# A two-block transformer kernel in fp32: the second feed-forward stage's output products by token tile, and h kept by token from there on

## The reference

```python
# first block
h = h + 0.5 * rmsnorm(swiglu(rmsnorm(h, g0), W_in0, W_out0), g1)     # stage "f0", inner width 2816
u = rmsnorm(h, g2)
h = h + rmsnorm(mlstm_mixer(u), g3)                                  # mixer "a", 8 heads
h = h + 0.5 * rmsnorm(swiglu(rmsnorm(h, g4), W_in1, W_out1), g5)     # stage "f1"; the 16 tokens are dropped
# second block, twice (layers 0 and 1)
shift, scale, gate = split(silu(c) @ w_ada[l] + b_ada[l])            # the modulation
u = rmsnorm(h, pre[l]) * (1 + scale) + shift
q, k, v, gates and convolution inputs = u @ w_in[l]
mix = concat(attention(q, k, v) * silu(g), short_conv(...) * silu(g2))
h = h + gate * rmsnorm(mix @ w_out[l], post[l])
```

## Time and profile before

| | |
|---|---|
| median of 3 runs | 803.59 us (802.58 to 805.04) |
| the profiled execution | 803.42 us, of it the span 801.6 us |
| PE, DVE, ACT, POOL busy | 791.0, 589.6, 419.3, 141.9 us |
| f1's output products, in the span | 469.07 to 530.32 us |
| boundary to layer 0's first product | 530.32 to 536.00 us |
| layer 0's query and key blocks, then values | 536.00 to 559.64, to 570.86 us |
| layer 0's output products, with the first tile's return | 640.89 to 666.37 us |
| layer 1's values, then query and key blocks | 666.37 to 680.80, to 703.58 us |

### The profile page before, as it was taken

How to read it: one execution, slowest core, us unless ns; L and a number is a source line. 1 busy time by engine, 2 the same in 40 slices (tenths; PEclk the granted TensorE clock), 3 DMA queues, 4 the chain that set the end, 5 groups by cost and what they waited for, 6 DMA issues and landing times.

```text
span 801.6 us, 15412 instructions
## 1 busy us (share of the span) xinstructions
PE 791.0 (99%) x6215; PEld 761.6 (95%) x6215; DVE 589.6 (74%) x938; ACT 419.3 (52%) x724; POOL 141.9 (18%) x155
## 2 busy tenths in 40 slices
PE   9999999999999999999999999999999999999997
PEld 9999999999999999999999999999899987999985
DVE  6877777699687976778777779996576667566753
ACT  7544444444358575555444455446546447556541
POOL 3800000042320000020000003330154411034510
PEclk9999999999899999999999999999999999999999
DMA  9876667695426642648867769555453560754531
GB/s 323 311 257 240 217 245 247 209 328 176 140 85 220 200 145 80 184 158 294 304 218 247 252 232 341 174 174 185 154 169 125 183 237 25 239 158 126 157 113 53
DMA packets 45190, 158.83 MB, mean 198 GB/s; under 512 B 5040, under 2 KB 6576, under 8 KB 45120
## 3 DMA queue, kind: packets, MB, share of 16 engines
q1 hardware_dynamic: 45120, 157.85, 59.4%
HBM read 156.76 MB, written 1.06 MB: 197 GB/s over the span
## 4 chain that ended last, share of the span: by engine, by line
PE 87%; DVE 9%; issue 2%; ACT 1%; POOL 0%; DVEq 0%; POOLq 0%; ACTq 0%
PE ps L334 24%; PE ps L336 23%; PE ps L335 23%; DVE w L1157 3%; PE ps L708 2%; DVE acc L1175 1%; PE ps L350 1%; PE ps L771 1%; PE ps L769 1%; PE ps L770 1%; PE ps L608 1%; PE ps L387 1%; PE ps L679 1%; PE ps L698 1%; PE ps L688 1%
## 5 line engine op out<-in xcount | busy, mean ns | idle before, releaser
L1157 DVE TENSOR_TENSOR w<-raw,w 128x1024 fp32r<-128x1024 f32 x241 | 295.9, 1240 | 136.3 <-ACT w L814 136.0
L334 PE MATMUL ps<-u,w 128*128 128x256 f32 (+1 forms) x1259 | 361.2, 287 | 0.6 <-DVE w L1157 0.6
L336 PE MATMUL ps<-u,w 128*128 128x256 f32 (+1 forms) x1259 | 357.6, 284 | 0.0
L335 PE MATMUL ps<-u,w 128*128 128x256 f32 (+1 forms) x1259 | 357.1, 284 | 0.0
L814 ACT CAST w<-raw 128x1024 fp32r<-128x1024 f32 x241 | 250.0, 1050 | 117.6 <-PE ps L336 103.4
L334 PEld LDWEIGHTS ps<-u,w 128*128 128x128 f32 x1259 | 237.5, 189 | 6.9 <-issue 4.3
L336 PEld LDWEIGHTS ps<-u,w 128*128 128x128 f32 x1259 | 237.8, 189 | 0.0
L335 PEld LDWEIGHTS ps<-u,w 128*128 128x128 f32 x1259 | 237.1, 188 | 0.0
L334 PE MATMUL ps<-h,w 128*128 128x272 f32 (+1 forms) x352 | 99.8, 283 | 0.0
L335 PE MATMUL ps<-h,w 128*128 128x272 f32 (+1 forms) x352 | 99.4, 282 | 0.0
L336 PE MATMUL ps<-h,w 128*128 128x272 f32 (+1 forms) x352 | 99.2, 282 | 0.0
(11 more groups left out here) (257 smaller groups left out, 957.3 us busy)
## 6 DMA issues: line engine op xcount, KB each, us to landing
raw<-wst SPq DMA_DIRECT2D x245, 512.0 KB, 4.6
adr<-wada SPq DMA_DIRECT2D x48, 512.0 KB, 4.1
Bt<-bias_rows SPq DMA_DIRECT2D x8, 192.0 KB, 3.9
hT<-xT SPq DMA_DIRECT2D x4, 272.0 KB, 5.4
outT<-hT SPq DMA_DIRECT2D x4, 256.0 KB, 2.0
cs<-cst SPq DMA_DIRECT2D x1, 140.0 KB, 6.4
cs<-cst SPq DMA_DIRECT2D x1, 128.0 KB, 6.9
vc<-vec SPq DMA_DIRECT2D x1, 101.0 KB, 3.6
```

What stands on the lines that cost most here:

```text
L334: e.matmul(out, a, x1, start=first, stop=False)
L335: e.matmul(out, a, x2, start=False, stop=False)
L336: return e.matmul(out, b, x1, start=False, stop=last)
L1157: e.tensor_tensor(b, raw[:, k % NRAW, :], a.bitcast(F32), ALU.subtract).then_inc(*tick(s_split, k))
```

## The change

f1's outputs are made by `token_outputs`, as a layer's are: the 22 blocks of the inner width are the stationary operand, 128 tokens at a time, and the rows of the second weight move, 512 columns in each half. 17 chunks are used for both token tiles, the last five in two passes. `ada_sums(1)` stands behind chunk 13, h is turned behind chunks 16 and 19. DVE's part of it is `second_ffn_out`, with the ten modulation steps and three folds at fixed chunks. The column sums, spreads and POOL's squares of f1 go, and with them `both_scales` and `normalised` of f1. `next_input` serves both boundaries. h is by token from f1's end; at layer 0's end it is read from SBUF (`ygf`) and not turned again. `attention(0)` now begins with its values, as `attention(1)` does; their four chunks are loaded inside f1's last chunks and lie in a new place, `side[0]`, over buffers of f1's modulation. Gain rows are made elsewhere: layer 0's `G2` in the boundary behind f0, f1's gains behind the mixer, both in the place of fillers; layer 1's `G2` at layer 0's start.

```diff
-        C_QK, C_G, C_V = (165, 209), (177, 217), ((173, 174, 175, 176), (202, 204, 206, 208))
-        C_OUT = ((197, 198, 199, 200, 201, 203, 205, 207), tuple(range(237, 245)))
+        C_QK, C_G, C_V = (169, 209), (177, 217), ((162, 164, 166, 168), (202, 204, 206, 208))
+        C_OUT = {"f1": (*range(143, 162), 163, 165, 167), "l0": (*range(197, 202), 203, 205, 207), "l1": (*range(237, 245),)}
...
-            def both_scales(s, n, rows_of_gains=False):
+            def both_scales(s, n):
...
                 spread(("r1", s), 6, n, rst)
-                if rows_of_gains:
-                    gain_rows(0, 1)
-                    rows_of_g2(0)
-                else:
-                    dense(6)
+                rows_of_g2(0, 0, 7)
+                dense(2)
                 e.wait_ge(s_pow.handle, at(s_pow, ("r2", s)))
                 spread(("r2", s), 5, n, rst2)
-                if rows_of_gains:
-                    dense(2)
-                    rows_of_g2(1)
+                dense(2)
+                rows_of_g2(0, 1, 4)
...
                 keys = [("in", 1, i) for i in range(2 * NF)]
-                head(keys[:4], C_F[1], x1, x2, S, *u_of("f1"), hook=spread_scale)
+                gain_rows("f1", 0, 7)
+                dense(2)
+                gain_rows("f1", 1, 4)
+                head(keys[:4], C_F[1], x1, x2, S, *u_of("f1"), fill=0, hook=spread_scale)
...
-                if l == 0:
-                    head(keys[:4], C_QK[0], x1, x2, S, *u_of("l0"), fill=0)
...
+                s = ("f1", "l0")[l]
+                values_of(0)
+                for half in range(2):
+                    gain_rows(("l0", "l1")[l], half)
                 if l == 0:
+                    rows_of_g2(1, 0, 4)
+                rows_to_features(s, 1, 0)
+                rows_to_features(s, 1, 1)
+                if l == 0:
+                    rows_of_g2(1, 1, 7)
+                values_of(1, 2)
+                for j in range(8):
+                    block(("qk", l, j), C_QK[l] + j, x1, x2, S)
...
-                early = KT - NW
-                for i in range(KT):
-                    e.wait_ge(s_split.handle, C_OUT[l][i] + 1)
+                early = n - NW
+                for i in range(n):
+                    e.wait_ge(s_split.handle, C_OUT[s][i] + 1)
                     products_of(i, 0)
                     if i < early:
                         products_of(i, 1)
-                    if l == 0 and i in (early - 1, 5):
-                        rows_of_h(i // 5)
-                def first_half_back():
-                    rows_to_features(0, 0)
-                    rows_to_features(0, 1)
-
-                for i in range(early, KT):
-                    products_of(i, 1, first_half_back if l == 0 and i == KT - 1 else None)
+                    if s == "f1" and i == early - 4:
+                        ada_sums(1)
+                    if s == "f1" and i in (early - 1, early + 2):
+                        rows_of_h(int(i > early))
+                for i in range(early, n):
+                    products_of(i, 1)
+                if s != "l1":
+                    rows_to_features(s, 0, 0)
+                    rows_to_features(s, 0, 1)
...
-            ffn_out(1, "f1", S)
-            both_scales("f1", S, True)
-            for l in range(2):
-                attention(l)
-                token_outputs(l)
+            token_outputs("f1")
+            attention(0)
+            token_outputs("l0")
+            attention(1)
+            token_outputs("l1")
...
+            rows_of(grow, ("grow", "f1"))
             ffn_in(1, S)
-            ffn_out(1, "f1", S)
-            gain_rows(0)
-            normalised("f1", S, shift_of(0))
...
+            split_to(C_V[0][0] - 1)
+
+            e.wait_ge(s_part.handle, at(s_part, (1, 2)))
+            split_to(C_V[0][3])
+            next_input("f1")
...
+            def second_ffn_out():
+                for i in range(NF):
+                    split_to(C_OUT["f1"][min(i + NW - 1, NF - 1)])
+                    while added[0] < {0: 41, 3: 43, 5: 44, 7: 46, 9: 48}.get(i, 0):
+                        ada_step(1)
+                    if i in (10, 11, 12):
+                        ada_fold(1, i - 10)
+                    if i == 14:
+                        modulation(1)
+                        layer_gains(1)
+                split_to(C_V[0][3])
...
+                        if l == 0:
+                            e.wait_ge(s_hrow.handle, at(s_hrow, (t, hf)))
+                            e.scalar_tensor_tensor(h, h, rst[:, t:t + 1], ps[:, bank_of(("hrow", t, hf)), :], ALU.mult,
+                                                   ALU.add).then_inc(*reading(("hrow", t, hf)))
+                        else:
+                            e.scalar_tensor_tensor(h, half_row(hTf, t, hf), rst[:, t:t + 1], h, ALU.mult, ALU.add).then_inc(
+                                *tick(s_htok, (t, hf)))
...
-            squares("f1", S)
-            boundary("f1", S)
+            next_scales("f1")
             attention(0)
```

More of the change, by code:

```diff
@@ L346, in block, with dense @@
                 last_of[c] = key
-            def dense(count):
+            def dense(count, b=4):
                 for _ in range(count):
-                    e.matmul(ps[:, 4, 0:256], dz[:, 0:128], dz[:, :], start=True, stop=True)
+                    e.matmul(ps[:, b, 0:256], dz[:, 0:128], dz[:, :], start=True, stop=True)
             def warm(count):
@@ L460, in ffn_out @@
                     for kt in range(NF):
-                        if j == KT - 1 and kt == (8 if n == T else NF // 2):
+                        if j == KT - 1 and kt == 8:
                             e.wait_ge(s_accy.handle, at(s_accy, (s, 6)))
@@ L528, in both_scales, with rows_of @@
                 e.wait_ge(s_pow.handle, at(s_pow, ("r2", s)))
                 spread(("r2", s), 5, n, rst2)
[L530 to L537 removed]
+                dense(2)
+                rows_of_g2(0, 1, 4)
+            def rows_of(columns, key, b, half):
+                b = place(key, b)
@@ L538, in rows_of_g2 @@
                 for j in range(4):
                     k = 4 * half + j
[L540 to L549, removed]
+                    m = e.transpose(ps[:, b, 128 * j:128 * j + 128], columns[:, k:k + 1].broadcast_to([P, P]), ident)
@@ new lines, in rows_of, with rows_of_g2, gain_rows @@
+                m.then_inc(*tick(s_grow, key))
+            def rows_of_g2(l, half, b):
+                e.wait_ge(s_G.handle, at(s_G, ("G", l)))
+                rows_of(G2[:, l, :], ("g2row", l, half), b, half)
+            def gain_rows(s, half, b=None):
+                if s == "f1":
+                    e.wait_ge(s_gh.handle, at(s_gh, 1))
+                else:
+                    e.wait_ge(s_G.handle, at(s_G, ("GP", int(s[1]))))
+                rows_of(GAIN[s], ("grow", s, half), b, half)
@@ L757, in attention, with token_outputs, products_of @@
                         block(("g", l, i), C_G[l] + i, x1, x2, S)
[L759 to L764, removed]
+            def token_outputs(s):
+                n = STEPS[s]
+                def products_of(i, t):
+                    if s == "f1":
+                        kt, parts = i, (h1[1], h2[1])
+                        e.wait_ge(s_h2.handle, at(s_h2, (1, kt)))
+                    else:
+                        l = int(s[1])
+                        kt, parts = ORDER[i], (m1[l], m2[l])
+                        e.wait_ge(s_m2.handle, at(s_m2, (l, kt)))
+                    x, y = (part[:, kt, 128 * t:128 * t + 128] for part in parts)
                     for hf in range(2):
-                        a, b = (w[:, 512 * hf:512 * hf + 512] for w in PLACE[C_OUT[l][i]])
-                        key = ("tok", l, t, hf)
+                        a, b = (w[:, 512 * hf:512 * hf + 512] for w in PLACE[C_OUT[s][i]])
+                        key = ("tok", s, t, hf)
                         out = ps[:, place(key) if i == 0 else bank_of(key), :]
@@ L770, in products_of @@
                         e.matmul(out, x, b, start=False, stop=False)
-                        e.matmul(out, y, a, start=False, stop=i == KT - 1).then_inc(*tick(s_proj, ("tok", l, i, t, hf)))
-                        if between and not hf:
-                            between()
+                        e.matmul(out, y, a, start=False, stop=i == n - 1).then_inc(*tick(s_proj, ("tok", s, i, t, hf)))
                     if t:
-                        last_of[C_OUT[l][i]] = ("tok", l, i, 1, 1)
-                early = KT - NW
-                for i in range(KT):
-                    e.wait_ge(s_split.handle, C_OUT[l][i] + 1)
+                        last_of[C_OUT[s][i]] = ("tok", s, i, 1, 1)
+                early = n - NW
+                for i in range(n):
+                    e.wait_ge(s_split.handle, C_OUT[s][i] + 1)
                     products_of(i, 0)
@@ L902, in mixer_out, with rows_of, normalised @@
                     e.mul(y, src, gain).then_inc(*reading(key))
[L904 to L910, removed]
```

(23 more changed lines are left out.)

309 lines of the change are left out of this document (131 added, 178 removed).

## The result

The changed kernel takes **806.65 us**, the median of 5 runs (806.06 to 807.35), against 803.59 (802.58 to 805.04) before: a ratio of 1.0037 [1.0025, 1.0049]. It is slower by 0.37%, and 0.45 us above the end of the forecast range. The profiled execution took 806.65 us (its span is 804.9), 3.2 above the one before.

A forecast was written before the change was run, and what follows sets the result against it. The prediction took TensorE, busy 99% of the span, as the bound. It summed +2.0 us (f1 through layer 0's query/key blocks) and -1.9 us (layer 0 to layer 1) to +0.1, forecasting 803.7 us, range 800.5 to 806.2.

The forecast's parts named there:

- The 512-column products: f1's output products: 264 of 512 columns at 0.2335 us each, 61.6 us against 59.7 for the old ones; no gain.
- The rival at 0.226: f1's 512-column products run at twice 0.113 us, 2.0 us less: 801.7, still no change; chance 0.09.
- The wait on the modulation: In f1 behind chunk 13, PE's modulation matmul waits for VectorE's last fold: PE stalls 1.7 us.
- VectorE's step 9 starts at 1.25: In f1, VectorE's step 9 starts 1.25 us after the end of chunk 8's products, following ScalarE's cast.
- what I cost at nothing: Transposes replacing fillers, ScalarE's extra copies, SP's reordered loads and the last modulation load in f1: no cost.
- If it came later, the fold would too, one for one: In f1, a late last modulation load delays VectorE's fold by the same time; no size was given.
- the new boundary: From f1 to layer 0: PE waits 0.7 us, values end at T+22.8 (T: first tile's products end), query/key blocks take 22.78.
- a rival at 0.11: PE's clock falls to half at the boundary behind f1, costing 3.4 us: slower, 807.1; chance 0.11.
- f1 to the end of the first tile: f1's products up to the first token tile's end, with modulation matmul, 1.7 stall and h's transposes: 58.2 us.
- Layer 0 to layer 1: Boundary between the layers: 16 transposes of h go (-1.6) and values end 0.4 sooner, with a 1.1 us wait: -1.9 us.
- Three waits not there: Rival: PE's waits of 1.7, 0.7 and 1.1 us at the fold and both boundaries vanish: faster, 800.2; chance 0.12.

The follow-up runs named there:

- the first experiment: The changed kernel with PE's modulation matmul behind chunk 15 of f1 instead of chunk 13: 801.0 us, 0.9969 of the kernel before.
- the fourth experiment: The changed kernel with the modulation matmul behind chunk 15, plus seven fillers at each of two places where h was transposed in layer 0's outputs: 802.49 us.

## Why the prediction was wrong

The forecast of no change failed by one wait, and by what came behind it.

- **The 512-column products: right.** They start every 0.233 to 0.234 us up to the wait; 39.20 us hold 168 of them (14 chunks x 12), 0.2333 each. The fixed 2.5 ns per matmul of the Trainium skill (page "TensorE: Matmul & The Clock Gate", section "Wait — 56ns, not 53.3ns?") does not show here: fewer, wider products were no faster, as the earlier trace rows had said. The rival at 0.226 is out, since two thirds of the products ran at 0.2333. But from the modulation's matmul on they ran at 0.229, in every trace of the changed kernel and its variants, whether the clock had been low or not; why is open.
- **The wait on the modulation: the mechanism was right, its size was off**, 4.20 us for 1.7. This is the term that failed. PE came to it at 507.83, 39.20 behind the start, exactly 14 chunks. VectorE's steps 10 to 12, from the split at 501.22 to the reduce's end at 511.93, took 10.7, as summed. What failed was "VectorE's step 9 starts at 1.25" and, under what I cost at nothing, "by the step times above it is issued some 5.6 us ahead of its use and lands in about 4.1". Chunk 8's products end at 468.63 + 108 x 0.2333 = 493.83, and step 9's split began at 494.82 + 1.14 = 495.96, that is at 2.13, 0.88 late behind steps that had waited for loads. Then the last load came 1.65 late: 4.8 us ahead, and 6.5 from issue to use. 0.88 + 1.65 = 2.5. I had taken the median landing of the whole kernel for a load that stood among weight chunks on the same queue, where the trace of before shows up to 6.6 us for the same loads in this stage; and I had named the rule that then holds ("If it came later, the fold would too, one for one") without a price.
- **What followed the wait: missed.** The clock at 0.50 from 512.40 to 515.81 held back nine products, eight of them 0.43 us apart and the last 0.30: 3.73 us for what takes 9 x 0.233 = 2.10, a cost of 1.6 us. I had this price only at the new boundary, as a rival at 0.11. There the clock held at 1.00 through all transposes and both waits, in every profiled execution. The fall came in a stage that I had read as dense.
- **f1 to the end of the first tile**: 62.2 us (468.63 to 530.81, 30 products ahead of 537.68) for 58.2. The excess of 4.0 is the wait's 2.5 and the clock's 1.6, within 0.1.
- **The new boundary: right.** Counted from that end, u's first values came at 538.78, 8.0 (forecast 8.1), the second tile's transposes at 546.30, 15.5 (15.6), the query/key blocks at 553.47, 22.7 (22.8), and these took 22.77. The wait there was 0.6 for 0.7: the last gain transpose starts at 545.63 and takes 0.11 of PE's time, and the next instruction starts at 546.30; the row's 0.40 counts from a modelled end.
- **Layer 0 to layer 1: right.** -2.16 for -1.9. The second tile's wait at 677.24 was 0.9 for 1.1, counted in the same way (from 676.21 + 0.11).
- **"Three waits not there": out.** All three were there.

Without the wait and the fall the first stretch comes to 107.61 - 4.20 - 1.6 = 101.8, what it was before, and the first experiment measured just that. The change then gains the 2.2 us between the layers, most of which the fourth experiment puts down to the transposes. What it lost was paid for one matmul's place.

Left open: whether the load on the DMA engines from 480 to 500 us is why the loads took so long there, and what brought the clock down behind the mixer; neither was tried. Nor was a version without the second tile's two waits, 1.5 us together.

## What to carry to other kernels

When work of another engine is pinned to steps of a loop, the place where the main engine needs its result has a price on both sides; move it by a step or two each way before judging the change around it. Cost a load that feeds such a chain by the landings of the loads in that stage (here 5.2 us in the median and up to 6.6, in the trace before the change), and not by the median of the whole kernel (4.1). And price an idle stretch of PE in a dense stage at more than its length: behind it the products may run at half clock.

## What the runs showed of the hardware that was not expected

- One idle stretch of 4.2 us, behind 39 us of dense products and followed by dense products, brought the clock to 0.50 for 3.41 us and cost 1.6 us more. Filled with 36 products of zeros, it did not (clock 1.00 from 500 to 530 us). An idle stretch of 1.9 us was followed by a fall in one profiled execution, one of 2.0 us in another was not: the length alone does not decide it in these runs.
- Transposes with short waits did not bring the clock down at the boundaries of f1 and layer 0 (1.00 over 15.79 and 14.25 us). The Trainium skill, same page, section "Part 4: PE-mode transpose", says that they do not count as PE being busy in the same way; the boundaries here do not bear it out, and the one fall behind the mixer does not either, since the clock was low 0.03 us after the first of the eight transposes there began.
- f1's products of 512 columns ran a little faster behind the modulation's matmul than ahead of it: 0.233 us each from 499.67 to 507.60 in the changed kernel, 0.228 from 529.89 to 531.26 (six in 1.37 us). The low clock is not the reason: with the matmul two chunks later the clock stayed at 1.00, and the pace changed at the matmul all the same. No run shows what the reason is.
